# A hybrid decoder step: the sample group's values read into the keys' slots, its queries sent between the keys, the output weights in memory of their own

## The reference, cut to what matters

```python
def dilated_sample(q, k_new, v_new, buf_k, buf_v, rel_bias):
    k_all = jnp.concatenate([buf_k, k_new], axis=1)      # 1024 cached keys and the new one
    v_all = jnp.concatenate([buf_v, v_new], axis=1)
    for (w, d) in ((128, 1), (512, 4), (2048, 16)):
        idx = L + t[:, None] - jnp.arange(w // d + 1)[None, :] * d
        kg, vg = k_all[:, idx], v_all[:, idx]
        logits = einsum('bthd,btjhd->bhtj', q, kg) * scale + bias    # softmax over j
        outs.append(einsum('bhtj,btjhd->bthd', p / den, vg))
    ...                                   # the branches are weighted by their denominators
mix = jnp.concatenate([o_a, o_d], axis=-1)
x = x + g1 * jnp.matmul(mix, w_o)
```

## Time and profile before

| | |
|---|---|
| median of 3 executions | 1364.57 us |
| the profiled execution's own time | 1368.63 us |
| its span (first to last instruction) | 1367.0 us |
| mean granted TensorE clock | 0.881 |
| busy in the span: PE, DVE, ACT, POOL | 80%, 42%, 36%, 9% |
| keys and spread queries on SP's queue | 630.5 to 663.0 us |
| values and `w_o` asked for | 674.9 to 695 us |
| stage 3 ends (DVE's copy at L1381) | 730.4 us |

### The profile page before, as it was taken

One profiled execution on the slowest core, in us unless ns is written; L12 is line 12 of the kernel. 1 busy time (PEld: TensorE's weight loads), 2 busy tenths in 40 slices (PEclk: granted clock), 3 DMA queues, 4 the chain that ended last, 5 costly groups with the idle time before them and its releaser, 6 DMA issues.

```text
span 1367.0 us, 19228 instructions
## 1 busy us (share of the span) xinstructions
PE 1092.3 (80%) x7177; PEld 608.6 (45%) x7178; DVE 576.1 (42%) x984; ACT 492.3 (36%) x824; POOL 123.5 (9%) x118
## 2 busy tenths in 40 slices
PE   4599849848999999999346999329999999999900
PEld 1255426534655555565213444214455554555400
DVE  1644233333232333323615665725544454445357
ACT  1433133124243333333112322325554564454334
POOL 0000000000000000000701001410001000010032
PEclk9799969858999999999657999659999999999965
DMA  9865210019121221106781212667988988979255
GB/s 335 294 225 188 52 47 0 1 45 329 31 77 42 62 64 40 49 13 170 203 245 25 76 68 71 185 247 257 383 292 277 357 303 285 355 253 335 103 200 187
DMA packets 128409, 231.42 MB, mean 169 GB/s; under 512 B 10491, under 2 KB 49176, under 8 KB 128183
## 3 DMA queue, kind: packets, MB, share of 16 engines
q1 hardware_dynamic: 114280, 195.01, 42.8%
q0 software_dynamic: 7168, 21.06, 4.6%
q10 hardware_dynamic: 6896, 14.45, 2.7%
HBM read 196.62 MB, written 33.87 MB: 169 GB/s over the span
## 4 chain that ended last, share of the span: by engine, by line
PE 35%; DVE 5%; DMA 5%; ACT 2%; issue 2%; SPq 1%; POOL 1%; POOLq 0%; DVEq 0%; ACTq 0%
PE banks L2051 8%; PE banks L1937 5%; PE banks L2015 4%; PE banks L2017 4%; PE banks L2016 4%; PE banks L2061 3%; PE banks L2074 2%; DMA arena<-in_w_o_dram 1%; DMA arena<-slot_rows,ids 1%; PE banks L2022 1%; PE banks L1973 1%; PE banks L2028 1%; POOL slot_token L746 1%; DVE arena L1373 1%; DMA arena<-h_rows,gidx 1%
## 5 line engine op out<-in xcount | busy, mean ns | idle before, releaser
L1518 DVE SCALAR_TENSOR_TENSOR arena<-arena 128x2048 f16<-128x2048 f32 x64 | 143.8, 2288 | 103.4 <-ACT arena L1037 103.4
L1656 PE MATMUL banks<-arena 128*128 128x384 f16 (+4 forms) x536 | 176.6, 329 | 1.4 <-DVE arena L1165 1.4
L1657 PE MATMUL banks<-arena 128*128 128x384 f16 (+4 forms) x536 | 176.1, 329 | 0.0
L1658 PE MATMUL banks<-arena 128*128 128x384 f16 (+4 forms) x536 | 176.0, 328 | 0.0
L1037 ACT ACTIVATE arena<-arena 128x2048 f16<-128x2048 f32 x64 | 118.9, 1911 | 47.8 <-issue 23.2
L2051 PE MATMUL banks<-arena 128*128 128x512 f32 x256 | 113.7, 597 | 0.0
L2015 PE MATMUL banks<-arena 128*128 128x512 f16 x256 | 97.9, 383 | 2.6 <-DVE arena L1546 2.6
L2016 PE MATMUL banks<-arena 128*128 128x512 f16 x256 | 97.9, 382 | 0.0
L2017 PE MATMUL banks<-arena 128*128 128x512 f16 x256 | 97.8, 382 | 0.0
L1937 PE MATMUL banks<-arena 128*128 128x512 f16 x384 | 90.5, 399 | 0.0
L942 ACT ACTIVATE arena<-arena 128x128 f32<-128x128 f32 (+7 forms) x96 | 53.5, 558 | 78.6 <-DVE arena L1295 78.5
(11 more groups left out here) (341 smaller groups left out, 1627.0 us busy)
## 6 DMA issues: line engine op xcount, KB each, us to landing
arena<-in_moe_w_gate_dram SPq DMA_DIRECT2D x32, 1024.0 KB, 6.3
arena<-in_moe_w_up_dram SPq DMA_DIRECT2D x32, 1024.0 KB, 9.0
arena<-in_moe_w_down_dram SPq DMA_DIRECT2D x16, 2048.0 KB, 12.5
arena<-in_w_ada_dram SPq DMA_DIRECT2D x12, 2048.0 KB, 12.0
arena<-in_w_in_dram SPq DMA_DIRECT2D x18, 512.0 KB, 5.8
slot_rows<-arena SPq DMA_DIRECT2D x2, 4096.0 KB, 20.8
slot_rows<-arena ACTq DMA_DIRECT2D x32, 256.0 KB, 7.3
out_dram<-arena SPq DMA_DIRECT2D x15, 512.0 KB, 3.3
```

What stands on the lines that cost most here:

```text
L1518: v.scalar_tensor_tensor(out=w_lo[s][p // 2][:, part], in0=stage[p], scalar=WS, in1=w_hi[s][p // 2][:, part], op0=ALU.mult, op1=ALU.subtra ...
L1656: mm(out, hTh[:, k, tok], wh(k), start=(first and k == ks[0]), stop=False)
L1657: mm(out, hTh[:, k, tok], wl(k), start=False, stop=False)
L1658: done = mm(out, hTl[:, k, tok], wh(k), start=False, stop=(last and k == ks[-1]))
```

## The change

1. **The values take the keys' slots** (`vC = kC`). The values of a sequence are asked for when DVE has summed that sequence's products (`slog_ok`), one sequence after another: 0 to 3 still in SP's part of stage 2, 4 to 7 after the barrier. Each half has a semaphore of its own (`vc_in[0]`, `vc_in[1]`), and each of PE's two rounds waits for its half.
2. **Queries between the keys.** SP sends keys 0 and 1, waits for `q_rows`, sends queries 0 and 1, and then keys and queries in turn.
3. **GpSimd signs the barrier of stage 2 ahead of its eight products** and waits for it behind them.
4. **Memory of their own for the quarters of `w_o`**, raw, high and low, in order of rows, with a semaphore each. ACT waits for the quarter it splits and for nothing of DVE's. The buffers of stage 4 move to other addresses.
5. **Masks ahead of splits.** DVE's order is mask 0, low part 0, mask 1, low parts 1 to 3.
6. Four semaphores of stage 1 (`gl_ps`, `z_ps`, `cum_ps`, `gT_ps`) become one (`gate_ps`) that counts to 4; the waits stand where they stood.

```diff
-        vC = [V(o_sa + b * 1536, 1536).rearrange("p (c n) -> p c n", c=2) for b in range(NB)]
+        vC = kC
...
-        o_raw = [o_late, A_T, A_T + 2 * D, A_T + 4 * D]
-        o_high = [o_late - 1536, o_late + 3 * D, o_late, A_T]
-        o_low = [o_late + 2 * D, o_late + D, A_T + D, A_T + 2 * D]
...
+        wO = [V(A_T + (6 + 2 * g) * D, 2 * D) for g in range(4)]
+        wOh = [V(A_T + (14 + 2 * g) * D, D).bitcast(F16) for g in range(4)]
+        wOl = [V(A_T + (15 + 2 * g) * D, D).bitcast(F16) for g in range(4)]
...
             sp.dma_start(q_rows, sqk[:, 0]).then_inc(gout, 16)
-            for b in range(4):
+            def load_q(b):
+                sp.dma_start(qB[b % 4], q_rows[b:b + 1].partition_broadcast(P)).then_inc(kc_in[b % 4], 16)
+            for b in range(2):
                 load_cache(kC[b], ck, b, kc_in[b])
             sp.wait_ge(gout, 16 * (HA + 4))
+            load_q(0)
+            load_q(1)
             sp.wait_ge(o_ps, 4 * (PAIRS - 1))
...
-            for b in range(4):
-                load_q(b)
-            for b in range(4, NB):
-                sp.wait_ge(sprod, b - 3)
+            for b in range(2, NB):
+                if b >= 4:
+                    sp.wait_ge(sprod, b - 3)
                 load_cache(kC[b], ck, b, kc_in[b % 4])
                 load_q(b)
+            for b in range(4):
+                sp.wait_ge(slog_ok, b + 1)
+                load_cache(vC[b], cv, b, vc_in[0])
             sp.wait_ge(kv_out, 32)
...
-            for b in range(NB):
-                load_cache(vC[b], cv, b, vc_in)
...
-            load_wO(0, KC - 2)
-            sp.wait_ge(slog_ok, NB)
-            for g in range(1, 4):
-                load_wO(g, 2 * g - 2)
+            for b in range(4, NB):
+                sp.wait_ge(slog_ok, b + 1)
+                load_cache(vC[b], cv, b, vc_in[1])
+            for g in range(4):
+                load_wO(g)
...
+            pool.drain().then_inc(stage_done, 1)
             for b in range(NB):
                 pool.wait_ge(kc_in[b % 4], 64 * (b // 4 + 1))
                 nc.gpsimd.tensor_tensor(kC[b], kC[b], qB[b % 4].unsqueeze(1).broadcast_to([P, 2, QW]), ALU.mult).then_inc(sprod, 1)
-            stage_end(pool, 2)
+            pool.wait_ge(stage_done, 5 * 2)
             stage_end(pool, 3)
...
-            act.wait_ge(wO_in, 64)
             for g in range(4):
-                if g >= 2:
-                    act.wait_ge(wlo_ok, 2 * PAIRS + 2 + (g - 1))
+                act.wait_ge(wO_in[g], 16)
                 A(wOh[g], wO[g], ACT.Copy, scale=WS).then_inc(whi_ok, 1)
...
+            mask(0)
+            low_wO(0)
+            mask(1)
+            for g in range(1, 4):
+                low_wO(g)
...
-            pe.wait_ge(vc_in, 48 * NB)
             for r in range(2):
+                pe.wait_ge(vc_in[r], 48 * 4)
```

More of the change, by code:

```diff
@@ L370, in build @@
         a1 = A_T
-        a1 += (KC - 2) * D
-        o_raw = [o_late, A_T, A_T + 2 * D, A_T + 4 * D]
-        o_high = [o_late - 1536, o_late + 3 * D, o_late, A_T]
-        o_low = [o_late + 2 * D, o_late + D, A_T + D, A_T + 2 * D]
[L375 to L378, removed]
+        wO = [V(A_T + (6 + 2 * g) * D, 2 * D) for g in range(4)]
+        wOh = [V(A_T + (14 + 2 * g) * D, D).bitcast(F16) for g in range(4)]
+        wOl = [V(A_T + (15 + 2 * g) * D, D).bitcast(F16) for g in range(4)]
+        assert A_T + 22 * D <= ARENA
         xr = [V(a1 + s * D, D) for s in range(2)]; a1 += 2 * D
-        h2 = [V(a1 + s * D, D) for s in range(2)]; a1 += 2 * D
+        sqj2 = V(a1, D); a1 += D
+        bcG1 = V(a1, D); a1 += D
         h2T = V(a1, D).rearrange("p (k n) -> p k n", k=KC); a1 += D
         rw = V(a1, KC * NE).rearrange("p (k n) -> p k n", k=KC); a1 += KC * NE
-        bcG1, bcA2, bcS2 = (V(a1 + i * D, D) for i in range(3)); a1 += 3 * D
-        sqj2 = V(a1, D); a1 += D
+        assert a1 <= A_T + 6 * D
+        a1 = A_T + 6 * D
+        h2 = [V(a1 + s * D, D) for s in range(2)]; a1 += 2 * D
+        bcA2, bcS2 = (V(a1 + i * D, D) for i in range(2)); a1 += 2 * D
         mixh, mixl = [], []
@@ L389, in build @@
         opart = h2[1]
-        assert a1 <= min(A_STAGE, o_late)
+        assert a1 <= A_T + 12 * D
         free = [[A_MOD, A_MOD + 2 * D], [A_CONST + _cols["oh"][0], A_CONST + _cols["oh"][0] + GN]]
@@ L449, in build @@
         wG_in = sem("wG_in"); gproj_ps = sem("gproj_ps"); gprojA = sem("gprojA"); gprojB = sem("gprojB")
[L450 to L451 removed]
+        gate_ps = sem("gate_ps"); gl_ok = sem("gl_ok"); lnz_ok = sem("lnz_ok"); loga_ok = sem("loga_ok")
+        edec_ok = sem("edec_ok"); scaled_ok = sem("scaled_ok");
         k2T_ok = sem("k2T_ok"); q4T_ok = sem("q4T_ok"); blk_ok = sem("blk_ok"); att_ps = sem("att_ps")
@@ L463, in build @@
         hT_hi = sem("hT_hi")
-        kc_in = [sem(f"kc_in{i}") for i in range(4)]; vc_in = sem("vc_in")
+        kc_in = [sem(f"kc_in{i}") for i in range(4)]; vc_in = [sem(f"vc_in{i}") for i in range(2)]
         self_ok = sem("self_ok"); slog_ok = sem("slog_ok"); sprod = sem("sprod")
@@ L467, in build @@
         smask_ok = sem("smask_ok")
-        wO_in = sem("wO_in")
+        wO_in = [sem(f"wO_in{i}") for i in range(4)]
         op_ps = sem("op_ps"); res_ok = sem("res_ok")
@@ L854, in _ @@
                 split_high_part(j, w0, w0h)
-            act.wait_ge(z_ps, 1)
+            act.wait_ge(gate_ps, 2)
             z = banks[:, 0:D]
@@ L862, in _ @@
             A(sT1, sT1, ACT.Ln, bias=C("one", NB)).then_inc(lnz_ok, 1)
-            act.wait_ge(cum_ps, 1)
+            act.wait_ge(gate_ps, 3)
             ed = Steps(act, edec_ok)
@@ L870, in _ @@
             ed.done(A(sA, sL, ACT.Exp), wait=False)
-            act.wait_ge(gT_ps, 1)
+            act.wait_ge(gate_ps, 4)
             A(k2T, banks[:, 0:D], ACT.Copy).then_inc(k2T_ok, 1)
@@ L1192, in _ @@
             cl.done(v.memset(oG[:, PT], 0.0), wait=False)
-            dve.wait_ge(gl_ps, 1)
+            dve.wait_ge(gate_ps, 1)
             dve.wait_ge(dve_link, lk.n)
@@ L1217, in _ @@
                     so.done(v.tensor_tensor(E3[e], src, E3[e], ALU.mult), wait=False)
-            dve.wait_ge(gT_ps, 1)
+            dve.wait_ge(gate_ps, 4)
             v.tensor_copy(q4T, banks[:, 1024:1024 + D]).then_inc(q4T_ok, 1)
@@ L1369, in _, with low_wO, mask @@
             v.tensor_tensor(pself, srow[:, CK:CK + 1].broadcast_to([n, NB]), C("seq8", n), ALU.mult).then_inc(sp_ok, 1)
-            for g in range(4):
+            def low_wO(g):
                 dve.wait_ge(whi_ok, 2 * PAIRS + 2 + (g + 1))
                 v.scalar_tensor_tensor(out=wOl[g], in0=wO[g], scalar=WS, in1=wOh[g], op0=ALU.mult, op1=ALU.subtract).then_inc(wlo_ok, 1)
-                if g < 3:
-                    dve.wait_ge(wlo_ok, 2 * PAIRS + 2 + (g + 1))
-            for r in range(2):
+            def mask(r):
                 dve.wait_ge(sov_ps, r + 1)
@@ L1683, in _ @@
                 tr(banks[0:RANK, t * P:(t + 1) * P], proj[:, t, 512:528], ident)
-            tr(bank(2, NB, RANK), proj[0:NB, PT, 512:528], ident[0:NB, 0:NB]).then_inc(gl_ps, 1)
+            tr(bank(2, NB, RANK), proj[0:NB, PT, 512:528], ident[0:NB, 0:NB]).then_inc(gate_ps, 1)
             pe.wait_ge(gl_ok, 2)
@@ L1689, in _ @@
                 mm(banks[:, t * P:(t + 1) * P], glT[0:RANK + 1, t * P:(t + 1) * P], wgu, start=True, stop=True)
-            mm(bank(2, P, NB), glT[0:RANK + 1, S:TOK], wgu, start=True, stop=True).then_inc(z_ps, 1)
+            mm(bank(2, P, NB), glT[0:RANK + 1, S:TOK], wgu, start=True, stop=True).then_inc(gate_ps, 1)
             pe.wait_ge(loga_ok, 2)
@@ L1696, in _ @@
                 last = mm(bank(6, PT)[:, t:t + 1], L[:, t * P:(t + 1) * P], C("ones")[:, 0:1], start=True, stop=True)
-            last.then_inc(cum_ps, 1)
+            last.then_inc(gate_ps, 1)
             pe.wait_ge(scaled_ok, 4)
@@ L1705, in _ @@
                 last = tr(banks[:, 2048 + t * P:2048 + (t + 1) * P], E[0][:, t * P:(t + 1) * P], ident)
-            last.then_inc(gT_ps, 1)
+            last.then_inc(gate_ps, 1)
             pe.wait_ge(k2T_ok, 1)
@@ L1920, in w_of @@
             def w_of(parts, k, h):
-                g = 0 if k >= KC - 2 else k // 2 + 1
+                g = k // 2
                 at = k % 2 * D + 512 * h
```

8 lines of the change are left out of this document (2 added, 6 removed).

## The result

The changed kernel took 1347.76 us (median of 1342.45, 1345.68, 1349.85 and 1350.79), the kernel before, beside it, 1365.59. The ratio is 0.9861, with a 95% interval from 0.9822 to 0.9901: 13.5 to 24.3 us less, where the forecast was 1344.3. Measured a second time, the changed kernel took 1345.27 against 1367.19, a ratio of 0.9851 (0.9824 to 0.9879). The profiled execution took 1345.68 us, with a span of 1344.0 and a granted clock of 0.888.

A forecast was written before the change was run, and what follows sets the result against it. The prediction took stage 3's DMA train and the work behind its end as the bound: 8.9 us from DMA holes plus 11.4 from a shorter tail, 20.3 off 1364.57, giving 1344.3 us; 8-in-10 range 1338 to 1353.

The forecast's parts named there:

- Which wait ends the stage: Stage 3 before: a DMA train whose last `w_o` quarter lands at 712.67, then 17.7 us of work behind it.
- The rival that SP's drain waits for its loads: Stage 2's barrier would open only as value 3 lands, at 681.0; 12.5 us off, 1352.1 us; chance 11%.
- The holes: Two gaps in DMA share, in 648 to 652 and 668 to 676, would close: 2.8 and 6.1 us, together 8.9.
- The rival that the values come at the rate of `w_o`: Values would move at 410 GB/s against 259, ending the stage at 702.9; 27.4 us off, 1337.2 us; chance 3%.
- The barrier: Stage 2's barrier no longer waits for GpSimd's product 8; expected between 661 and 669.3, taken as 664.
- The last sum: DVE needs 2.1 us after the barrier, then 6.71 for the last four sums: all done at 673.
- The second round: PE's second pass over the values starts with value 7 at 693.8, takes 8.2 us and ends at 702.0.
- the first rival: PE's clock already up, so its second pass takes 4 to 6.4 us, not 8.2: 1342.2 us; chance 10%.
- the cover of 2.0 to 7.2 us: Slack in stage 3 between the end of PE's first pass, by 691.8, and value 7's landing.
- What sets the end: Stage 3: DVE's three low parts behind mask 1 end at 709.8, the copy at 710.1; last `w_o` quarter's branch at 708.0.
- The rival of the lower clock: Stage 4's `w_o` projections run at 1.2 GHz; three of them would make it 10.8 us slower, 1375.4; chance 6%.
- Nothing: Merged semaphores wait where they waited and new addresses change no shape, so these parts were expected to have no effect.

The follow-up runs named there:

- Masks behind: Changed kernel with DVE's old order again, low parts 0 to 3 and then masks 0 and 1: 1351.61 us, ratio 0.9899.
- one wait: Changed kernel, but ACT waits for all four quarters of `w_o` before it splits the first: 1353.12 us, ratio 0.9904.
- queries behind the keys: Changed kernel with the spread queries again sent after the first four sequences of keys: 1351.74 us, ratio 0.9884.
- halves: Changed kernel with keys 0 and 1 loaded before the query rows and the last quarter of `w_o` loaded and split in two: 1342.38 us, ratio 0.9822.
- values behind: Changed kernel with values 0 to 3 asked for after the barrier, GpSimd still signing early: 1347.07 us, and 1344.10 us when run again.
- late sign: Changed kernel with GpSimd again signing the barrier of stage 2 after its eight products: 1342.62 us, ratio 0.9831.

## Why the prediction was right, point by point

- **Which wait ends the stage.** Right: the train and the tail behind it. Both parts were confirmed by undoing them, and neither PE nor stage 4 took the gain back. The rival that SP's drain waits for its loads falls: SP asked for value 3's last rows at 661.59 and the barrier opened at 664.4, while no DMA of that line (L577, from 650 on) landed in less than 8.0 us, that is before 669.6:

```profile
DMA to landing us min/median/max: 8.0/11.7/17.9
```

- **GpSimd's start and its last product.** 641.2 and 671 forecast, 640.42 and 670.81 measured.
- **The holes.** 8.9 us forecast; the train ended 11.15 earlier. About 1.0 of the 2.3 us beyond are three shallower dips of the kernel before that the forecast left out, a share of 0.86, 0.95 and 0.94 in 652 to 660 and 676 to 680 (4 x 0.14 + 4 x 0.05 + 4 x 0.06), where the changed kernel has 1.03 or 1.04. The deepest of them, in the windows before:

```profile
652.00:656.00 4.00, 0.84 (x4) 0.53 (x6) 3.85 (x7) 1.73 (x5) 4.00 (x2) 0.71 0.86 278
```

The rest fits the rate at full share, which differs between executions: among the runs without a hole and with the same requests from keys to `w_o` the last quarter was there between 71.4 and 73.2 us after the query rows, and the changed kernel's trace, with 71.4, is the earliest of them. That this trace beat the forecast so clearly is partly luck. The rival that the values come at the rate of `w_o` falls: they moved at 253 to 281 GB/s from 664 to 688.
- **The barrier.** 664 forecast, 664.4 measured, set by SP: DVE had been done since 662.1, 2.28 us earlier. The forecast took 664 out of a range from 661 to 669.3, so that the number fits this closely is partly luck.
- **The last sum.** 673 forecast, 677.56 measured. Here a size was off: the 2.1 us for DVE's own product and sum ahead of the last four sums were 6.5 (664.39 to 670.85). Nothing was lost, since `w_o`, asked for behind the last sum at 678.91, still came before the engines ran dry.
- **The second round.** Forecast 8.2 us after a pause, measured 5.9 after a pause of 0.24, as the first rival had it: in the window around it the granted clock was 0.69, a mean of its lower level (0.50, 1.2 GHz) and its higher (2.4 GHz). The pause was that short because softmax and first round ended late, at 691.3, and the last value came early, at 691.5 instead of 693.8; the cover of 2.0 to 7.2 us was all but gone (and with values 0 to 3 there at 681.0, as forecast, it could not have been above 693.8 - 681.0 - 8.2 = 4.6). But the pause alone doesn't decide. Masks behind, after 3.48 us of pause, and one wait, after 0.80:

```profile
690.46 3.64 PE L1902 MATMUL banks<-arena 128*32 128x512 f32 x16 [3.48 <-DMA arena<-in_cache_win_v_dram]
...
696.17 0.62 PE L1906 MATMUL banks<-arena 8*12 8x256 f32 x8
```

```profile
693.26 3.64 PE L1904 MATMUL banks<-arena 128*32 128x512 f32 x16 [0.80 <-DMA arena<-in_cache_win_v_dram]
...
700.53 1.04 PE L1908 MATMUL banks<-arena 8*12 8x256 f32 x8
```

The round took 6.3 us after the longer pause and 8.3 after the shorter, though one wait changes nothing that PE does up to there. What decides when the clock rises is open, and so is whether the change or chance made the round quick.
- **What sets the end.** Forecast: DVE's low parts behind mask 1, at 710.1, with the last quarter's branch done 2 us before that. Measured: both together. The quarter's branch ends at 703.45 + 2.29 = 705.74, DVE's three back-to-back low parts at 705.78. Where one of the two is late, it alone decides: DVE's low parts with a slow second round (queries behind the keys) or an earlier train (halves). The forecast had low part 0 done before the second round; it was done 0.7 us behind it (698.17 for 697.46), and mask 1 waited for it.
- **The sum.** Trace: 24.5 us at the copy for 20.3 forecast, less 1.5 behind it. The train gave 2.3 us more than forecast (11.15 for 8.9) and the tail 1.9 more (13.3 for 11.4), the latter from the quicker second round. Time: 17.8 us by the first medians, 21.9 by the second pair. The profile before stood 3.0 us over its median of 1365.59 and the profile after 2.1 under its own, which is why the spans differ by more than the medians. So the mechanism and the order of events are right; that the times lie on both sides of the forecast 20.3 us, while the trace gave more at the copy, is partly luck.
- **Stage 4.** The rival of the lower clock is out: the granted clock is 1.00 in the windows from 712 to 740, and the first two projections by `w_o` take 10.53 us each, as before (10.54 and 10.53). The first of them, in PE's timeline after:

```profile
715.65 10.53 PE L1938 MATMUL banks<-arena 128*128 128x512 f16 x48
```

- **Nothing.** No run undoes the merged semaphores or the new addresses alone. The query rows' store at 630.11 for 629.95, and what lies behind the copy, show no effect of them beyond what differs between the runs.

## What to carry to other kernels

Where a full train of DMAs decides, look for the windows in which its share falls, and ask what each first request after the hole waited for; here one early request or one early sign was enough to close the second hole, and the other bought nothing. Then shorten what follows the last landing: wait by part, and put on an in-order engine whatever is ready first, since the order that was best for one arrival time leaves it idle at another. Take the gain from the medians of runs made side by side: in one profile alone the same kernel's train ended up to 2.7 us earlier or later (values behind, 76.0 and 73.3).

## What was not expected of the hardware

**DVE was held up by GpSimd.** L1350, 8x96, takes 0.24 us when GpSimd is done (late sign) and took 3.03 beside a product that ran from 667.39 to 670.81; it ended at 670.92. L1348 took 2.49 us for 0.95, and ended 0.8 us behind the product that ended at 666.08. DVE's sums over one input, beside products too, kept their 1.73 to 1.74 us. The Trainium skill (SBUF — State Buffer, Who interferes with whom) says that a DVE instruction with two SBUF inputs contends with a GpSimd instruction that reads SBUF, and that this contention is an exclusive lock. The trace agrees: both instructions ended within 0.15 us of the product's end plus their own time.

**The same loads run at different rates with all engines full.** Rows of 3 KB moved at 231 to 243 GB/s in one execution (values behind), at 251 to 267 in another of the same kernel, at 260 to 275 in the changed kernel, all from 676 to 688; `w_o` moved at 410 in each. No run here shows what sets this; it is as large as the effects of single edits in a trace.
